# The condition's weight slots of a two-layer decoder step: inside the feed-forward products, or at the boundaries between sub-layers

## What is computed

```python
def _layer(x, c, l, prm, past):
    ada = jax.nn.silu(c) @ prm['w_ada'][l] + prm['b_ada'][l]      # D -> 9 D
    ada = ada.reshape(B, N_SUB, 3, D)[:, :, :, None, :]
    def pre(j, z):
        return _rmsnorm(z, prm['g_pre'][l, j]) * (1 + ada[:, j, 1]) + ada[:, j, 0]
    def post(j, z, y, w):
        return (z + w * (1 + ada[:, j, 2]) * _rmsnorm(y, prm['g_post'][l, j])).astype(z.dtype)
    x = post(0, x, _swiglu(pre(0, x), prm['w_ffn_in'][l, 0], prm['w_ffn_down'][l, 0]), FFN_RES)
    y, st = _mix(pre(1, x), l, prm, past)
    x = post(1, x, y, 1.0)
    x = post(2, x, _swiglu(pre(2, x), prm['w_ffn_in'][l, 1], prm['w_ffn_down'][l, 1]), FFN_RES)
```

## Time and profile before

| | |
|---|---|
| three runs | 1905.34, 1912.64, 1914.37; median 1912.64 |
| profiled execution | 1915.48; its span 1913.4; mean granted clock 0.967 |
| TensorE matmul busy | 1777.3 (93%) |
| TensorE weight load busy | 1541.9 (81%, overlaps the former) |
| VectorE / ScalarE / GpSimd busy | 1038.4 (54%) / 776.6 (41%) / 82.6 (4%) |
| transfers | 391.90 MB, mean 205 GB/s |

### The profile page before, as it was taken

How to read it: one execution, slowest core, us unless ns; L and a number is a source line. 1 busy time by engine, 2 the same in 40 slices (tenths; PEclk the granted TensorE clock), 3 DMA queues, 4 the chain that set the end, 5 groups by cost and what they waited for, 6 DMA issues and landing times. The chain is left out here.

```text
span 1913.4 us, 33255 instructions
## 1 busy us (share of the span) xinstructions
PE 1777.3 (93%) x12776; PEld 1541.9 (81%) x12776; DVE 1038.4 (54%) x1867; ACT 776.6 (41%) x1413; POOL 82.6 (4%) x111
## 2 busy tenths in 40 slices
PE   5999989999999997999959989899999899979997
PEld 3888878877876786998859879688778667869997
DVE  3555454566567635654355543556665675266554
ACT  3554344344433204654344543443445221056552
POOL 0000010000000001000010000100000000010001
PEclk8999989999999998999979999899999999989998
DMA  8678635536348732556537786255453596325651
GB/s 322 255 300 316 230 129 201 197 147 239 145 156 304 263 110 98 185 197 260 228 131 286 270 306 241 103 227 189 146 224 139 192 331 222 125 96 175 233 222 53
DMA packets 85951, 391.90 MB, mean 205 GB/s; under 512 B 12472, under 2 KB 17856, under 8 KB 55488
## 3 DMA queue, kind: packets, MB, share of 16 engines
q1 hardware_dynamic: 72816, 368.24, 52.6%
q10 hardware_dynamic: 13008, 21.94, 3.2%
HBM read 377.32 MB, written 12.83 MB: 204 GB/s over the span
## 5 line engine op out<-in xcount | busy, mean ns | idle before, releaser
L1046 DVE TENSOR_TENSOR ring_parts<-ring,pages_parts 128x1024 fp32r<-128x1024 f32 (+1 forms) x272 | 314.4, 1192 | 204.1 <-ACT pages_parts L1626 204.0
L534 PE MATMUL ps<-arena_parts,pages_parts 128*128 128x264 f32 x1408 | 364.1, 293 | 27.4 <-DVE xn_parts L1114 21.4
L535 PE MATMUL ps<-xn_parts,pages_parts 128*128 128x264 f32 x1408 | 358.8, 289 | 0.0
L1626 ACT ACTIVATE pages_parts<-ring 128x1024 fp32r<-128x1024 f32 (+1 forms) x272 | 267.8, 1025 | 186.8 <-DMA ring<-in_w_ffn_in 77.5
L534 PEld LDWEIGHTS ps<-arena_parts,pages_parts 128*128 128x128 f32 x1408 | 272.6, 194 | 48.0 <-issue 47.4
L535 PEld LDWEIGHTS ps<-xn_parts,pages_parts 128*128 128x128 f32 x1408 | 271.7, 193 | 0.0
L495 PE MATMUL ps<-xn,ring 128*128 128x264 f32 x896 | 212.6, 394 | 6.0 <-ACT xn L1633 6.0
L495 PEld LDWEIGHTS ps<-xn,ring 128*128 128x128 f32 x896 | 170.3, 193 | 39.8 <-issue 6.8
L539 PE MATMUL ps<-arena_parts,ring_parts 128*128 128x264 f32 x1408 | 197.0, 283 | 0.0
L534 PE MATMUL ps<-big_parts,pages_parts 128*128 128x264 f32 x704 | 177.7, 288 | 7.4 <-DVE gates_parts L1060 6.6
L539 PEld LDWEIGHTS ps<-arena_parts,ring_parts 128*128 128x128 f32 x1408 | 181.2, 188 | 0.0
(11 more groups left out here) (334 smaller groups left out, 2586.7 us busy)
## 6 DMA issues: line engine op xcount, KB each, us to landing
ring<-in_w_ffn_in SPq DMA_DIRECT2D x88, 1024.0 KB, 5.0
ring<-in_w_ada SPq DMA_DIRECT2D x32, 1536.0 KB, 6.6
ring<-in_w_a SPq DMA_DIRECT2D x32, 1536.0 KB, 7.5
ring<-in_w_ffn_down SPq DMA_DIRECT2D x32, 1408.0 KB, 6.7
pages<-in_k_pages SPq DMA_DIRECT2D x128, 256.0 KB, 5.6
pages<-in_v_pages SPq DMA_DIRECT2D x128, 256.0 KB, 4.0
ring<-in_w_ada SPq DMA_DIRECT2D x24, 1024.0 KB, 7.4
ring<-in_w_proj SPq DMA_DIRECT2D x8, 1536.0 KB, 9.4
```

The costliest lines, as they stand in the source:

```text
L534: mm(ps[:, b, 0:T], tile, hi[:, k, :], start=start, stop=False)
L535: return mm(ps[:, b, 0:T], tile, lo[:, k, :], start=False, stop=False)
L1046: v.tensor_tensor(ring_lo[:, r, at * P:(at + n) * P], w, whi[:, place, 0:n * P].bitcast(F32), ALU.subtract)\
L1626: A(whi[:, place, 0:n * P], ring[:, r, at * P:(at + n) * P], ACT.Copy).then_inc(S.whi_ready, 1)
```

## The change

- The down-projection of the first feed-forward carries no condition slots any more and takes the plain loop `down(1)`. Its four wide slots form a group at boundary 1: slot 0 ahead of `post_sum(1)`, 1 and 2 behind it, 3 behind `pre_sums(2)`.
- The four narrow slots of the second feed-forward's input form the same kind of group at boundary 2. `first_ffn_slot` now stands once, ahead of the loop, and the loop holds 16 plain slots.
- In `down_with_next` the last three slots move behind chunk 7, with `post_sum(3)` after the first of them; VectorE's row copy for them moves into `residual(3)`.
- `Slots.group()` gives the ring places of a group: the three places behind the weight held for the time after the boundary (`held`), and for the fourth the first of them again. SyncE loads held weight, group, and then the rest.
- The transposes and the add of a group follow behind the first products after the boundary. `A_SLOTS` follows the new ring position.

Layer 0 has eleven such slots (4 + 4 + 3), layer 1 eight (4 + 4). No computation, load or product is added or left out. Core of the diff:

```diff
-ADA_AFTER = (0, 2, 4, 5)
-NEXT_AFTER = ((0, 1), (1, 2), (2, 3), (3, 4), (4, 5), (5, 6), (6, 8), (8, 8))
+NEXT_AFTER = ((0, 1), (1, 2), (2, 3), (3, 4), (4, 5), (5, 5), (5, 5), (5, 8))
-A_SLOTS, A_FREE = (1, 2, 1, 3), 0
+A_SLOTS, A_FREE = (2, 1, 2, 3), 0
+    def group(self):
+        first = self.pos
+        four = [self.take(1) for _ in range(3)] + [self.take(1, first)]
+        self.pos = (first + 1) % SLOTS
+        return four
...  SyncE
-                    if c in ADA_AFTER:
-                        load(ins.w_ada12[layer, 12 + ADA_AFTER.index(c)], 1)
-                for s in range(2):
-                    load(ins.w_sq[layer, s], 2)
+                load(ins.w_sq[layer, 0], 2)
+                load_group(ins.w_ada12[layer, 12:16])
+                load(ins.w_sq[layer, 1], 2)
...
+                load(ins.w_ffn_in[layer, 1, 0], 2)
+                load_group(ins.w_ada8[layer, 8:12])
                 with sp.Fori(0, 4) as i, slots.loop(i, 4, [2] * 4):
                     for k in range(4):
-                        load(ins.w_ffn_in[layer, 1, i * 4 + k], 2)
-                for k in range(16, FC):
+                        load(ins.w_ffn_in[layer, 1, i * 4 + k + 1], 2)
+                for k in range(17, FC):
                     load(ins.w_ffn_in[layer, 1, k], 2)
-                    if k < 20:
-                        load(ins.w_ada8[layer, k - 8], 1)
...  TensorE, down_with_next
                         for q in range(*NEXT_AFTER[c]):
                             ada_slot(q % 4, 8)
+                            if q == 5:
+                                post_sum(3)
...  TensorE, boundary 1
-                down_with_ada()
+                down(1)
+                held, group = slots.take(2), slots.group()
+                ada_slot(0, 12, group[0])
                 post_sum(1)
+                ada_slot(1, 12, group[1])
+                ada_slot(2, 12, group[2])
                 pre_sums(2)
+                ada_slot(3, 12, group[3])
...
                 for s in range(2):
-                    r = open_slot(2)
+                    r = open_slot(2) if s else full(held)
                     product(r, 0, xn_of if s else xn_as_it_comes, KC)
                     product(r, KC, xn_of, KC)
+                    if s == 0:
+                        ada_columns(ada0 + 3, 12)
...  TensorE, boundary 2
+                held, group = slots.take(2), slots.group()
+                ada_slot(0, 8, group[0])
                 post_sum(2)
+                ada_slot(1, 8, group[1])
+                ada_slot(2, 8, group[2])
                 pre_sums(3)
+                ada_slot(3, 8, group[3])
+                first_ffn_slot(2 * KC, held)
+                ada_columns(ada0 + 4, 8)
                 with pe.Fori(0, 4) as i, slots.loop(i, 4, [2] * 4), products.count.loop(i, 4, 8), \
                         pieces.count.loop(i, 4, 8):
-                    first_ffn_slot(2 * KC)
-                    for k in (1, 2, 3):
+                    for k in range(4):
                         ffn_slot()
...
-                    post_sum(3)
                     ada_columns(ADA_GROUPS + 1, 8)
...  VectorE
                 for s in range(2):
                     slots.take(2)
+                    if s == 0:
+                        ada_copy(slots.group()[3], 12)
...
+                ada_copy(group[3], 8)
+                ffn_slot(0, 0, held)
+                ada_columns(ada0 + 4, 8, ADA_N - 8)
...
+                        if c == 5 and between:
+                            between()
```

More of the change, by code:

```diff
@@ L353, in load, with load_group, fill @@
                 def load(src, parts, at=None):
+                    fill(src, slots.take(parts, at))
+                def load_group(first):
+                    for q, slot in enumerate(slots.group()):
+                        fill(first[q], slot)
+                def fill(src, slot):
                     tiles = src.shape[-1] // P
-                    r, _, before = slots.take(parts, at)
+                    r, _, before = slot
                     sp.wait_ge(slot_done[r], before + 1)
@@ L482, in open_slot, with full @@
                 def open_slot(parts, at=None):
-                    r, loads, _ = slots.take(parts, at)
+                    return full(slots.take(parts, at))
+                def full(slot):
+                    r, loads, _ = slot
                     pe.wait_ge(slot_full[r], loads * 16 + 16)
@@ L503, in sample_rows, with ada_slot @@
                     return last
-                def ada_slot(q, group):
+                def ada_slot(q, group, slot=None):
                     cols = group // 4 * P
-                    r = open_slot(1)
+                    r = open_slot(1) if slot is None else full(slot)
                     if q == 0:
@@ L561, in ffn_slot, with first_ffn_slot @@
                     ffn_products(open_slot(2))
-                def first_ffn_slot(before):
-                    r = open_slot(2)
+                def first_ffn_slot(before, slot=None):
+                    r = open_slot(2) if slot is None else full(slot)
                     places = []
@@ L1018, in ada_rows, with ada_copy @@
                     for q in range(4):
-                        r, _, before = slots.take(1)
+                        slot = slots.take(1)
                         yield
+                    ada_copy(slot, group)
+                    yield
+                def ada_copy(slot, group):
+                    r, _, before = slot
                     dve.wait_ge(slot_done[r], before + 2)
@@ L1115, in split_input, with residual @@
                                             ALU.subtract).then_inc(S.xn_ready, 1)
-                def residual(n):
+                def residual(n, between=None):
                     dve.wait_ge(S.yrs_ready, n)
@@ L1137, in down @@
                         sum_squares()
[L1139 to L1154, removed]
                 def down_with_next():
@@ L1173, in down_with_next @@
                             ada_columns(ADA_GROUPS, 8, 0)
+                    return rows_of
                 if first_layer:
@@ L1554, in _ @@
                 split_input(3, xhi, xlo)
+                held, group = slots.take(2), slots.group()
+                ahead.group()
+                split(2 * KC)
+                ada_copy(group[3], 8)
+                ffn_slot(0, 0, held)
+                ada_columns(ada0 + 4, 8, ADA_N - 8)
                 with dve.Fori(0, 4) as i, slots.loop(i, 4, [2] * 4), ahead.loop(i, 4, [2] * 4), \
@@ L1664, in down @@
                         y_chunk(r, before + 2, c)
-                def down_with_ada():
-                    for c in range(KC):
-                        if c in ADA_AFTER:
-                            ahead.take(1)
-                        if c < KC - 1:
-                            split(FC)
-                        r, _, before = slots.take(1)
-                        y_chunk(r, before + 2, c)
-                        if c in ADA_AFTER:
-                            slots.take(1)
                 def down_with_next():
@@ L1732, in _ @@
                         slots.take(1)
-                down_with_ada()
+                down()
                 post(1)
@@ L1743, in _ @@
                 ahead.follow(slots)
-                for s in range(2):
-                    ahead.take(2)
+                ahead.take(2)
+                ahead.group()
+                ahead.take(2)
                 at, free = ahead.places()
@@ L1763, in _ @@
                     r, _, before = slots.take(2)
+                    if s == 0:
+                        slots.group()
                     for n in range(2):
@@ L1941, in _ @@
                 modulate(3)
+                ahead.group()
+                split(2 * KC)
+                ffn_slot(0, 0)
+                slots.group()
                 with act.Fori(0, 4) as i, slots.loop(i, 4, [2] * 4), ahead.loop(i, 4, [2] * 4), \
                         products.count.loop(i, 4, 8), pieces.count.loop(i, 4, 8), exps.loop(i, 4, 4), link.loop(i, 4, 8):
-                    for k in range(4):
+                    for k in range(1, 5):
                         split(2 * KC)
                         ffn_slot(k, i * 4 + k)
-                for k in range(16, FC):
-                    if k < 20:
-                        ahead.take(1)
+                for k in range(17, FC):
                     split(2 * KC if k < FC - 1 else FC)
                     ffn_slot(k, k)
-                    if k < 20:
-                        slots.take(1)
                 if last_layer:
```

40 lines of the change are left out of this document (9 added, 31 removed).

## The result

The changed kernel takes 1886.3 us (median; 1879.5 to 1899.8) against 1911.2 us before; ratio 0.989, 95% interval 0.987 to 0.991. The forecast was 1887 us, ratio 0.987, range 1877 to 1898. The two medians of the first comparison lie 24.9 us apart; its ratio puts the gain at 21.6 us (17.6 to 25.6), that of the second at 21.0. The sum said 25.3.

The account below looks back on a forecast made before the run. TensorE was taken as the bound, waiting only at sub-layer boundaries. Terms -27.3 + 0.4 + 2.6 - 1.0 = -25.3 us took the profiled 1915.5 to 1890.2, the median from 1912.6 to 1887.3; range 1877 to 1898.

Parts of the forecast that it names:

- The sum: Whole launch: -27.3 taken out, +0.4 for slot 0, +2.6 for slot 2, -1.0 for the clock, giving -25.3 us.
- Narrow slots and stalls: Eleven 256-column slots leave second feed-forward inputs and layer 0's down-projection, 12.9 us saved; two late weight splits, 1.6 us saved.
- Wide slots: Eight 384-column slots leave the first feed-forwards' down-projections: 1.6 us each, 12.8 us saved.
- Boundary 1: After the first feed-forward's down-projection: slot 0 delays the post-norm sum 0.2 us, late slot 2 costs 1.0, per layer.
- Boundary 2: After the output projection: slot 2, landing late before the pre-norm sums, costs 0.3 us each time.
- Clock: Less idle time before w_sq products and first feed-forward slots may keep full clock: 1.0 us saved, ends 0 and 8.
- the forecast's floor of 14.9: The four w_sq products cannot take less than 14.9 us; they took 16.9 in layer 0.
- The rival of the full clock: Boundaries keep full clock, so neither slot 2 nor the first products lose: about 1880 us; chance 0.15.
- Covers: w_a's first slot is split over 8 us before use; w_ffn_in's thinner store costs 0, at most 2 us per layer.
- boundary 3's row copy: End of layer 0: VectorE's row copy inside the residual costs 0, at most 0.5 us.
- Slower: Narrow products leave the clock at 0.50 behind the four filled boundaries; 10 us per boundary give 1921; chance 0.02.
- hidden: A load, ScalarE or VectorE sets the pace once the slots are gone, no gain: 1915 us; chance 0.04.

Follow-up runs that it names:

- e6: Kernel before, condition slots in place, with unread products of the same shape added in the waits of boundaries 1 and 2; ratio 0.998 (0.997 to 1.000).
- e1: Kernel before with only the four wide slots of each layer moved, to boundary 1; ratio 0.995 (0.993 to 0.997).
- e4: The whole changed kernel again, against the kernel before (the second comparison); 1889.0 against 1909.5 us, ratio 0.989 (0.986 to 0.992).
- e8: Changed kernel with the moved slots' products cut to 4 columns and 14 of 32 matmuls per group; ratio to before 0.988 (0.986 to 0.990).
- e10: Changed kernel with boundary 1's four condition slots loaded in plain order ahead of both w_sq weights; ratio to before 0.987 (0.985 to 0.990).
- e11: Changed kernel with slot 2 put behind the pre-norm sums at both boundaries, loads unchanged; ratio to before 0.984 (0.982 to 0.987).
- e9: Changed kernel with the first down-projection on TensorE written out instead of a loop; 1881.0 us, ratio to before 0.984 (0.982 to 0.987).
- e7: Kernel before with the nineteen slots' products cut in place to 4 columns and 14 of 32 matmuls per group; ratio 0.996 (0.995 to 0.998).
- e5: Kernel before run again unchanged, for a second profile of it; ratio 1.001 (0.999 to 1.003).

## Why the forecast was right, and where its terms were off

- *Narrow slots and stalls.* Said: 4.7 us per input 2, 0.8 more for layer 1's stall, 4.2 for down 2. Measured in the four profiles of the table: 4.8 to 5.7 in layer 0, 5.9 to 6.5 in layer 1, 4.05 in down 2; no thinner supply of w_ffn_in, no new wait. Right. (Layer 1's stall is not in every execution of the old order: e6 and e1 had none.)
- *Wide slots* are the step that was mis-sized. Said: 71.59 - 64.85 = 6.74 us less per down-projection. The price of the slots was right (70.70 to 63.95 where the clock held), but the plain form that it was read from is a loop, and the wait before its start was not looked at: TensorE enters the loop only behind the wait, 1.95 instead of 1.55 us, and in most cases the clock then falls and takes 1.5 us. In the twelve first down-projections of e1, e4, e8, e10, e11 and after that the change made into loops, nine had the fall. That is 0.4 + 0.75 x 1.5, or 1.5 us per layer, 3 in all; e9 shows it by taking it away (63.95 us behind 1.55 in both layers). The profile of before had shown one such loop, without the fall, and the 1.97 us wait before it.
- *Boundary 1.* Said: +0.2 and +1.0. Measured over the six passages of after, e1 and e4, 17.19 us on average against 16.14: +1.05. The post-norm sum itself came 0.1 late, not 0.2. The load issued as the last chunk ended landed 6.2 us later in layer 0 and 6.4 in layer 1 (forecast 6.4), and full or half clock at slot 2 made the difference, as argued: 0.1 us at full clock, 0.8 to 1.05 where the clock fell there for 3.4 us, 2.2 where it fell for 6.8 (layer 1 of e4). The 5.6 us estimated from the Trainium skill ("DMA: Bandwidth & Descriptors", "Anatomy of one DMA") stays short of the rows here too. e8, e10 and e11 confirm the mechanism from three sides.
- *Boundary 2.* Said: +0.3 each; it was 0.0.
- *Clock.* Said: 1 us in all. In nine of ten passages the w_sq products went from 15.8 to 17.1 to 14.4 (without the transposes), 1.4 us or more per layer; the forecast's floor of 14.9 for them was too high. The rival of the full clock was half right: the fall before the w_sq products is gone, that at other places is not. In what is paid out, this nearly offsets the loss at the loops.
- *Covers.* w_a's first slot was issued at 270.78 and split from 277.16 on, well before its use at 287.02; boundary 3's row copy cost nothing.
- *Slower, hidden.* Neither showed. e7 shows, however, that the argument against "hidden" was too narrow: it looked at a down-projection with no condition loads in it. With the products alone gone, waits behind those loads grow by 6.3 us, a quarter of the 23.8 that the slots take in place. The change moves the loads as well, and in its profiles these waits are gone.

Summed over the stages, waits included, the touched ones give 26.3 us between the profiles of before and e5 and those of after and e4, and 25 if each stage is averaged over all profiles that have it in either form. In both sums the loss at the last down-projection is taken off: 1 us on average, since its clock fell in all seven loops that follow the new input 2 and in two of the six behind the old. The timed gain is 21.6 (17.6 to 25.6). What lies between 21.6 and 25 is within the interval; the profiles show no stage that takes it, and it stays open.

That the forecast of 1887 came within 1 us of the median is in part luck. Two errors, 3 us too little for the loops and 2 us too little for the clock at the w_sq products, nearly cancelled, and the median of four runs can lie several us to either side.

## What to carry to other kernels

Work moved into a wait must have its data there when the wait begins: a load that needs the ring place just left comes a whole landing time later, so put such a piece behind the work that is ready in between. Price a plain form from its first wait to its last instruction, loop entry and clock included. Before crediting a product's time, ask whether the next load is as late as the product is long; a version with the product cut down in place tells, if the waits that grow in its place are counted too.

## What the runs showed of the hardware

- Entering a loop on TensorE behind a semaphore wait lengthened the wait by 0.40 us (1.93 to 1.97 against 1.54 to 1.55), and the granted clock fell to half for 3.4 us behind 18 of 25 such entries, which cost 1.5 us each, and behind none of the 31 written-out starts.
- Products of 4 columns in the waits (e8) kept the w_sq products at full clock as wide ones did (14.7 us), though the clock fell before the sums. What in the waits decides it is not settled: the changed order with no product at all in its waits was not tried.
- Products late by 1.2 us were made up before the last square came, though the granted clock was 0.56 in 262.7 to 269.5 (e8, layer 0: sums from 5.60 to 11.01 us behind the post-norm sum; in the kernel before from 4.41 to 11.01).
- Between executions the mixer, whose products no kernel here changed, took 429.6 to 440.5 us, and one kernel's runs spread over some 1%. Parts worth 2 to 10 us could be told only by stage.
